# The up-products of MLP and feed-forward layers as 512-column products in two PSUM banks

## The chip, the core and the metric

The kernel runs on one core of one Trainium2 chip. A core has TensorE (PE in the profile; its weight loads are the separate row PEld), VectorE (DVE), ScalarE (ACT), GpSimd (POOL) and SyncE (SP), and DMA engines that bring data from memory. The metric is the time of one execution in microseconds on the device; less is better.

## The reference, cut to what matters

A stack of four blocks (a sequence mixer and an MLP each) is followed by two layers (feed-forward, hybrid mixer, cross attention, feed-forward), on 256 tokens of width 1024, all in float32. The change concerns the first product of each MLP and the gate and up products of each feed-forward:

```python
D_MODEL = 1024; SEQ = 256; D_FF = 4 * D_MODEL; D_FF_2 = 2816
def sq_relu_mlp(h, w1, w2):                      # four times, h is (256, 1024)
    return jnp.square(jax.nn.relu(h @ w1)) @ w2
def swiglu(h, w_gate, w_up, w_down):             # four times
    return (jax.nn.silu(h @ w_gate) * (h @ w_up)) @ w_down
    ...
for i in range(DEPTH):       # 4
    x = x + rms_norm(mixer(rms_norm(x, norm_g[i, 0])), norm_g[i, 1])
    h = rms_norm(x, norm_g[i, 2])
    x = x + rms_norm(sq_relu_mlp(h, mlp_w1[i], mlp_w2[i]), norm_g[i, 3])
for l in range(DEPTH_2):     # 2
    x = x + 0.5 * swiglu(rms_norm_2(x, ffn1_norm[l]), ffn1_w_gate[l], ffn1_w_up[l], ffn1_w_down[l])
    x = x + hybrid_mixer(...)
    x = x + memory_cross_attention(...)
    x = x + 0.5 * swiglu(rms_norm_2(x, ffn2_norm[l]), ffn2_w_gate[l], ffn2_w_up[l], ffn2_w_down[l])
```

## The kernel before

Activations lie with channels on the 128 partitions and the 256 tokens along the free side, as 8 chunks of 128 channels. To keep float32 accuracy with the faster number format of TensorE (fp32r), each operand is split in a high and a low part, and a product is the sum of three: high weights with high activations, high weights with low activations, low weights with high activations. Low with low is left out.

Weights stream through the core in slabs of 128 x 2048 numbers (1 MB). For each slab SP issues the DMA into `ring` (3 places; a place is free when the slab three before it has its low part, line 405), ACT copies it rounded into `wH` (line 1440; 2 places, free when the products of the slab two before are done, line 1439), and DVE takes the difference `wL` (line 2064). PE multiplies. The order on every engine is written out by hand in one function per layer kind, and semaphores join the engines: `high_split`, `low_split` (a slab's parts are there), `products_done` (its products are done), `bank_read` (its PSUM bank has been read).

An MLP has 16 up slabs and 16 down slabs, a feed-forward 22 up slabs (half gate, half up columns of 128) and 11 down slabs. The first two up slabs are done by `first_products`, in step with the arrival of the normalized activations; the change does not touch them. It touches slabs 2 to 15 of each of the four MLPs and slabs 2 to 21 of each of the four feed-forwards: 4 x 14 + 4 x 20 = 136 slabs. Each of them gives two column blocks of 128 channels x 256 tokens, which fill the halves of one PSUM bank (4 + j % 4). For each block `three` (line 602) issues 8 products high x high, 8 high x low, 8 low x high, each 256 columns wide with a weight load of its own: 48 products per slab.

Behind the product, in an MLP: ACT makes the ReLU of the bank into `act_s` (line 1578), DVE multiplies it with the bank into `prod_s` (the square, line 2175, which frees the bank), ACT rounds it to the high part of the hidden activations (line 1595), and DVE takes their low part (line 2164). In a feed-forward: DVE scales the bank by the row norm into `act_s` (line 2220, frees the bank), ACT makes SiLU of the gate half (line 1600), DVE multiplies the halves (line 2204), ACT rounds (line 1604), DVE takes the low part (line 2209). On ACT and DVE, the split of the slab two further on stands ahead of this work: in `ready` (line 1449) and `refill` (line 2075). The down products then use banks 0 to 3 (`down_product`).

## Time and profile before

| | |
|---|---|
| time, median of 3 runs | 2692.18 us (2687.8 to 2705.8) |
| span of the profiled execution | 2705.3 us (the longest of the three times, 2705.8, is 0.5 us above it) |
| PE busy | 2625.5 us, 97% of the span, 21582 products |
| weight loads busy | 2553.7 us, 94% |
| DVE busy | 1660.7 us, 61% |
| ACT busy | 1351.4 us, 50% |
| POOL busy | 152.2 us, 6% |
| chain that ended last | PE 85%, DVE 6%, ACT 4% |
| mean granted clock of TensorE | 0.993 |

The page gives busy time by engine, the busy share in 40 slices of the span, the DMA queues, the chain of work that ended last (followed back from the end), and the costliest groups of instructions with their mean duration and the idle time before them. A product of TensorE is pipelined: the time from one start to the next is what it costs in a row of products, and its own duration is longer.

### The profile page before, as it was taken

To read this page: it belongs to the slowest core of one execution; us is meant where nothing else is said; L and a number is where in the kernel's file an instruction comes from. 1 tells how busy PE (TensorE), PEld (TensorE's weight loads), DVE (VectorE), ACT (ScalarE), POOL (GpSimd) and SP (SyncE) were. 2 spreads that over 40 slices of the span, in tenths; PEclk is the share of its full clock that TensorE was granted. 3 is DMA by queue.
4 is the path that set the end of the run, shared out by engine and by line. 5 is a ranking of instruction groups with operands and counts; after the bars stand their busy time and mean duration, and the time that the engine had idled before them with its cause. 6 is when DMAs were issued, how large, how long until landed. Compare 5 with 4: busy or idle time off the path is not lost.

```text
span 2705.3 us, 48788 instructions
## 1 busy us (share of the span) xinstructions
PE 2625.5 (97%) x21582; PEld 2553.7 (94%) x21582; DVE 1660.7 (61%) x1970; ACT 1351.4 (50%) x1663; POOL 152.2 (6%) x224
## 2 busy tenths in 40 slices
PE   8989999999998999989999999999999999999998
PEld 8979999899997999988999999989999999999998
DVE  5657655475575754676755665766665657764664
ACT  5645545454436544663544444554545446544543
POOL 4400000000000000330000000000000000000000
PEclk9999999999999999999999999999999999999999
DMA  7514564456643565442565756434766655334663
GB/s 214 162 33 141 187 234 133 152 176 211 211 144 121 179 219 186 144 147 94 171 216 178 191 187 211 152 125 141 196 194 187 189 199 159 126 130 142 188 188 125
DMA packets 429970, 451.96 MB, mean 167 GB/s; under 512 B 13346, under 2 KB 395024, under 8 KB 427584
## 3 DMA queue, kind: packets, MB, share of 16 engines
q1 hardware_dynamic: 417952, 416.12, 49.2%
q0 software_dynamic: 7312, 32.35, 3.5%
q8 instruction: 170, 2.79, 0.4%
q10 hardware_dynamic: 4496, 0.39, 0.1%
q14 instruction: 40, 0.33, 0.0%
HBM read 441.21 MB, written 7.60 MB: 166 GB/s over the span
## 4 chain that ended last, share of the span: by engine, by line
PE 85%; DVE 6%; ACT 4%; POOL 2%; DMA 1%; issue 1%; ACTq 0%; SPq 0%; DVEq 0%
PE ps L593 85%; ACT wH L1440 2%; DVE wL L2064 2%; POOL arena L497 1%; ACT hidden_parts L1500 1%; PE ps L1037 0%; POOL arena L499 0%; DMA ring<-in_gdn_w_in 0%; DVE arena L2484 0%; DMA arena<-tiles_out 0%; DVE arena L2592 0%; DMA arena<-leaf_out 0%; DMA leaf_out<-arena 0%; POOL arena L507 0%; DVE arena L2335 0%
## 5 line engine op out<-in xcount | busy, mean ns | idle before, releaser
L2064 DVE TENSOR_TENSOR wL<-ring,wH 128x2048 fp32r<-128x2048 f32 x392 | 898.4, 2292 | 781.2 <-ACT wH L1440 780.8
L1440 ACT ACTIVATE wH<-ring 128x2048 fp32r<-128x2048 f32 x392 | 752.4, 1919 | 1050.6 <-PE ps L593 1048.6
L593 PE MATMUL ps<-hidden_parts,wH 128*128 128x256 f32 x6656 | 1005.0, 279 | 4.1 <-ACT hidden_parts L1500 2.7
L593 PEld LDWEIGHTS ps<-hidden_parts,wH 128*128 128x128 f32 x6656 | 910.8, 188 | 6.1 <-issue 3.6
L593 PE MATMUL ps<-hidden_parts,wL 128*128 128x256 f32 x3328 | 700.4, 279 | 1.0 <-DVE wL L2064 1.0
L593 PEld LDWEIGHTS ps<-hidden_parts,wL 128*128 128x128 f32 x3328 | 525.4, 188 | 1.4 <-DVE wL L2064 1.4
L593 PE MATMUL ps<-hH,wH 128*128 128x256 f32 x2624 | 369.5, 282 | 7.1 <-DVE hH L2081 5.0
L593 PE MATMUL ps<-hH,wL 128*128 128x256 f32 x2624 | 361.6, 279 | 2.2 <-DVE wL L2064 2.2
L593 PEld LDWEIGHTS ps<-hH,wH 128*128 128x128 f32 x2624 | 331.4, 189 | 16.6 <-issue 15.9
L593 PE MATMUL ps<-hL,wH 128*128 128x256 f32 x2624 | 347.0, 278 | 0.0
L593 PEld LDWEIGHTS ps<-hH,wL 128*128 128x128 f32 x2624 | 329.2, 189 | 2.9 <-DVE wL L2064 2.8
L593 PEld LDWEIGHTS ps<-hL,wH 128*128 128x128 f32 x2624 | 322.1, 188 | 0.0
L593 PE MATMUL ps<-arena 128*128 128x128 f32 (+1 forms) x1392 | 231.0, 312 | 21.1 <-ACT arena L1840 7.5
L593 PEld LDWEIGHTS ps<-arena 128*128 128x128 f32 x1392 | 197.0, 195 | 40.1 <-ACT arena L1840 10.2
L593 PE MATMUL ps<-sq,onesR 128*128 128x256 f32 (+1 forms) x216 | 71.8, 461 | 4.8 <-ACT sq L1516 2.8
L2320 DVE SCALAR_TENSOR_TENSOR hT<-hT,arena 128x255 f32<-128x255 f32 (+1 forms) x144 | 60.9, 492 | 3.7 <-ACT hT L1660 3.4
L2220 DVE TENSOR_TENSOR arena<-ps,rs 128x512 f32<-128x512 f32 x88 | 60.2, 684 | 0.1
L593 PEld LDWEIGHTS ps<-sq,onesR 128*128 128x128 f32 x216 | 37.3, 189 | 19.7 <-issue 8.0
L593 PE MATMUL ps<-hidden_parts 128*128 128x256 f32 x384 | 53.3, 291 | 0.0
L593 PEld LDWEIGHTS ps<-hidden_parts 128*128 128x128 f32 x384 | 49.0, 191 | 0.9
L2175 DVE TENSOR_TENSOR arena<-arena,ps 128x512 f32<-128x512 f32 x64 | 43.6, 681 | 5.9 <-ACT arena L1578 5.9
L1595 ACT ACTIVATE hidden_parts<-arena 128x512 fp32r<-128x512 f32 x64 | 40.1, 627 | 12.1 <-DVE arena L2175 12.1
(301 smaller groups left out, 1965.2 us busy)
## 6 DMA issues: line engine op xcount, KB each, us to landing
ring<-in_mlp_w SPq DMA_DIRECT2D x128, 1024.0 KB, 5.4
ring<-in_ffn_w_gate SPq DMA_DIRECT2D x88, 512.0 KB, 3.9
ring<-in_ffn_w_up SPq DMA_DIRECT2D x88, 512.0 KB, 5.2
ring<-in_ffn_w_down SPq DMA_DIRECT2D x44, 1024.0 KB, 5.0
ring<-in_gdn_w_in SPq DMA_DIRECT2D x32, 1024.0 KB, 5.9
ring<-in_w_in SPq DMA_DIRECT2D x28, 1024.0 KB, 5.4
hidden_parts<-mem_parts POOLq DMA_DIRECT2D x14, 1024.0 KB, 7.5
ring<-in_mlstm_w_in SPq DMA_DIRECT2D x12, 1024.0 KB, 5.2
```

The lines of the kernel that those rows point to most:

```text
L497: W.chain(pool.tensor_tensor(step, leafA[:, k, k + 1:LEAF][:, :, None].broadcast_to([P, n, c]), leafX[:, k, 0:c][:, None, :].broadcast_to( ...
L593: return pe.matmul(o, l, r, start=start, stop=stop, **k)
L1440: f(wH[:, n % PARTS, :], ring[:, n % RING, :], ACT.Copy).then_inc(sem("high_split"), 1)
L1500: ins = f(x_parts[0][:, k, :], xT[:, k, :], ACT.Copy, scale=column(gain, k0 + k))
L1595: f(hidH[:, 2 * g:2 * g + 2, :], two(prod_s[:, g % 2, :]), ACT.Copy).then_inc(sem("hiddenH_ready"), 1)
L2064: tt(wL[:, n % PARTS, :], ring[:, n % RING, :], wH[:, n % PARTS, :].bitcast(F32), ALU.subtract)\
L2175: tt(prod_s[:, g % 2, :], act_s[:, g % 2, :], ps[:, 4 + g % 4, :], ALU.mult)\
L2220: tt(two(act_s[:, n % 2, :]), two(ps[:, 4 + n % 4, :]), rs_twice(), ALU.mult)\
L2320: ins = stt(dst, src, w, dst, ALU.mult, ALU.add)
```

## The change

Slabs 2 and on of the up-products take two PSUM banks each, in turns of three pairs (0 and 1, 6 and 7, 4 and 5), one bank per column block. Bank halves no longer stand for column blocks: the left half collects high weights x high activations, the right half high weights x low activations. As both use the same weights, one product of 512 columns does both, with an operand that steps over the high and the low tensor (so `hH` and `hL` become the two halves of one tensor `normed`). The low weights then go over the high activations alone into the left half. A slab has 16 products of 512 columns and 16 of 256.

The halves must be added. In an MLP ACT copies the right halves out of both banks (in place of ReLU), DVE adds the left halves to the copy (frees the banks), and, after the low part of the slab before, makes max(x, 0) times x in one instruction from the sum. In a feed-forward ACT has a new copy of the right halves into `sum_s`, DVE has a new addition, and the scaling reads the sum. New semaphores tell that the square (`hidden_squared`) and the scaled units (`units_scaled`) are there. PE waits for the pair's bank_read from slab 5 on, for `hidden_squared` or `units_scaled` at slab 4, and for the banks of the last but one slab before the down product. The wait that the memory filler's bank (6) has been emptied stands at slab 3 in place of 2. The load of the identity at the start signals the semaphore of x. The core of the diff:

```diff
-        hH = sb("hH", [P, DC, T], F32R)
-        hL = sb("hL", [P, DC, T], F32R)
+        normed = sb("normed", [P, 2, DC, T], F32R)
+        hH, hL = normed[:, 0, :, :], normed[:, 1, :, :]
...
+        sum_s = A.take(2 * 512, "p (b n) -> p b n", b=2)
...
+        ffn_both = hidden_parts[:, :, 24:32, :]
...
+        def wide_banks(j):
+            return (0, 6, 4)[(j - 2) % 3]
+
+        def both_sums(j):
+            v = ps[:, wide_banks(j):wide_banks(j) + 2, :]
+            return v[:, :, 0:T], v[:, :, T:2 * T]
... PE
+            def wide_product(u, j, high_of, low_of, x):
+                for m in range(2):
+                    bank = wide_banks(j) + m
+                    halves = two(ps[:, bank, :])
+                    for k in range(DC):
+                        mm(halves, high_of(k, m), x[:, :, k, :], k == 0, False, skip_group_check=True)
+                    if m == 0:
+                        pe.wait_ge(sem("low_split"), u + 1)
+                    for k in range(DC):
+                        last = mm(ps[:, bank, 0:T], low_of(k, m), x[:, 0, k, :], False, k == DC - 1,
+                                  skip_group_check=True)
+                last.then_inc(sem("products_done"), 1)
... PE, mlp
                 for j in range(2, 16):
-                    if j == 2:
+                    if j == 3:
                         filler_out(filled_before[("mlp", i)])
-                    to_channels("mlp_w1", i, j, bank_of(j), free="bank_read")
+                    if j == 4:
+                        pe.wait_ge(sem("hidden_squared"), W.next("hidden_squared", 2))
+                    if j >= 5:
+                        pe.wait_ge(sem("bank_read"), W.next("bank_read"))
+                    u = slab_no[("mlp_w1", i, j)]
+                    wh, wl = high(u, DC), low(u, DC)
+                    wide_product(u, j, lambda k, m: columns(wh, k, m), lambda k, m: columns(wl, k, m), normed)
...
+                W.next("hidden_squared", 14)
+                pe.wait_ge(sem("bank_read"), W.next("bank_read", 2))
 
                 def floor():
-                    pe.wait_ge(sem("bank_read"), W.next("bank_read", 4))
+                    pe.wait_ge(sem("bank_read"), W.next("bank_read"))
                     norm_floor()
... ACT, mlp
-                    f(act_s[:, g % 2, :], ps[:, 4 + g % 4, :], ACT.Relu).then_inc(sem("act_ready"), 1)
+                    src = two(ps[:, 4 + g, :]) if g < 2 else both_sums(g)[1]
+                    f(two(act_s[:, g % 2, :]), src, ACT.Copy).then_inc(sem("act_ready"), 1)
... ACT, ffn
                     ready(kind, l, n)
+                    if n >= 2:
+                        f(two(sum_s[:, n % 2, :]), both_sums(n)[1], ACT.Copy).then_inc(sem("act_ready"), 1)
... DVE, mlp
-                    tt(prod_s[:, g % 2, :], act_s[:, g % 2, :], ps[:, 4 + g % 4, :], ALU.mult)\
-                        .then_inc(sem("bank_read"), 1)
+                    src = act_s[:, g % 2, :]
+                    if g >= 2:
+                        tt(two(src), both_sums(g)[0], two(src), ALU.add).then_inc(sem("bank_read"), 1)
                     if g >= 1:
                         hidden_low(g - 1)
+                    if g >= 2:
+                        dve.wait_ge(sem("bank_read"), W.next("bank_read"))
+                    stt(prod_s[:, g % 2, :], src, 0.0, src, ALU.max, ALU.mult).then_inc(sem("hidden_squared"), 1)
... DVE, ffn
-                    tt(two(act_s[:, n % 2, :]), two(ps[:, 4 + n % 4, :]), rs_twice(), ALU.mult)\
-                        .then_inc(sem("bank_read"), 1)
-                    dve.wait_ge(sem("bank_read"), W.next("bank_read"))
+                    src = ps[:, 4 + n, :] if n < 2 else sum_s[:, n % 2, :]
+                    if n >= 2:
+                        dve.wait_ge(sem("act_ready"), W.next("act_ready"))
+                        tt(two(src), both_sums(n)[0], two(src), ALU.add).then_inc(sem("bank_read"), 1)
+                        dve.wait_ge(sem("bank_read"), W.next("bank_read"))
+                    tt(two(act_s[:, n % 2, :]), two(src), rs_twice(), ALU.mult).then_inc(sem("units_scaled"), 1)
+                    dve.wait_ge(sem("units_scaled"), W.next("units_scaled"))
```

What stands in a row on PE for one up slab of the first MLP (slab 4), before:

```order
L593 MATMUL ps<-hH,wH 128x256 [waits mlp_bank_read,high_split]
L593 MATMUL ps<-hH,wH 128x256 x7
L593 MATMUL ps<-hL,wH 128x256 x8
L593 MATMUL ps<-hH,wL 128x256 [waits low_split]
L593 MATMUL ps<-hH,wL 128x256 x7
L593 MATMUL ps<-hH,wH 128x256 x8
L593 MATMUL ps<-hL,wH 128x256 x8
L593 MATMUL ps<-hH,wL 128x256 x8
```

and for the same slab now (`normed` holds hH and hL):

```order
L602 MATMUL ps<-normed,wH 128x512 [waits high_split,hidden_squared]
L602 MATMUL ps<-normed,wH 128x512 x7
L602 MATMUL ps<-normed,wL 128x256 [waits low_split]
L602 MATMUL ps<-normed,wL 128x256 x7
L602 MATMUL ps<-normed,wH 128x512 x8
L602 MATMUL ps<-normed,wL 128x256 x8
```

The six groups of eight became four, the wait for the low weights comes after 8 wide products in place of 16 narrow ones, and the wait for the bank is one for an event later in the work on DVE.

On DVE, up slabs 3 and 4 of the first MLP, before (line 2064 is the low part of a slab two further on, 2175 the square, 2164 the low part of the hidden activations):

```order
L2064 TENSOR_TENSOR wL<-ring,wH 128x2048 [waits high_split]
L2175 TENSOR_TENSOR arena<-arena,ps 128x512 [waits act_ready,hidden_ready]
L2164 TENSOR_TENSOR hidden_parts<-arena,hidden_parts 128x512 [waits hiddenH_ready]
L2064 TENSOR_TENSOR wL<-ring,wH 128x2048 [waits high_split]
L2175 TENSOR_TENSOR arena<-arena,ps 128x512 [waits act_ready,hidden_ready]
L2164 TENSOR_TENSOR hidden_parts<-arena,hidden_parts 128x512 [waits hiddenH_ready]
```

and now (2096 the low part of a slab, 2209 the addition, 2196 the low hidden part, 2214 the square):

```order
L2096 TENSOR_TENSOR wL<-ring,wH 128x2048 [waits high_split]
L2209 TENSOR_TENSOR arena<-ps,arena 128x512 [waits act_ready,hidden_ready]
L2196 TENSOR_TENSOR hidden_parts<-arena,hidden_parts 128x512 [waits hiddenH_ready]
L2214 SCALAR_TENSOR_TENSOR arena<-arena 128x512 [waits mlp_bank_read]
L2096 TENSOR_TENSOR wL<-ring,wH 128x2048 [waits high_split]
L2209 TENSOR_TENSOR arena<-ps,arena 128x512 [waits act_ready,hidden_ready]
```

One instruction of 128x512 has been added per slab, and the square now stands last. The release of PSUM stays where it was, directly behind the low part of the slab.

## Rows read from the trace of the kernel before

**Rows 1.** The page: busy time, and the chain that ended last.
```profile
PE 2625.5 (97%) x21582; PEld 2553.7 (94%) x21582; DVE 1660.7 (61%) x1970; ACT 1351.4 (50%) x1663; POOL 152.2 (6%) x224
...
PE ps L593 85%; ACT wH L1440 2%; DVE wL L2064 2%; POOL arena L497 1%; ACT hidden_parts L1500 1%; PE ps L1037 0%; POOL arena L499 0%; DMA ring<-in_gdn_w_in 0%; DVE arena L2484 0%; DMA arena<-tiles_out 0%; DVE arena L2592 0%; DMA arena<-leaf_out 0%; DMA leaf_out<-arena 0%; POOL arena L507 0%; DVE arena L2335 0%
```

**Rows 2.** Waits in total, times, longest (us).
```profile
ACT wH L1440 <- PE ps L593: 1048.6, 348, 6.8
DVE wL L2064 <- ACT wH L1440: 780.8, 333, 8.0
...
PE ps L593 <- DVE wL L2064: 5.0, 7, 1.6
```

**Rows 3.** Timeline, PE, first MLP, up slabs: start, length (us), count.
```profile
262.31 1.10 PE L593 MATMUL ps<-hH,wH 128*128 128x256 f32 x8
...
273.62 1.10 PE L593 MATMUL ps<-hH,wH 128*128 128x256 f32 x8
```

**Rows 4.** Timeline, second MLP, a steady up slab, three engines.
```profile
619.73 1.07 PE L593 MATMUL ps<-hH,wH 128*128 128x256 f32 x8
620.01 1.92 ACT L1440 ACTIVATE wH<-ring 128x2048 fp32r<-128x2048 f32 x1 [2.51 <-PE ps L593]
...
621.83 0.59 ACT L1578 ACTIVATE arena<-ps 128x512 f32<-128x512 f32 x1
621.97 2.29 DVE L2064 TENSOR_TENSOR wL<-ring,wH 128x2048 fp32r<-128x2048 f32 x1 [1.95 <-ACT wH L1440]
...
624.18 0.68 DVE L2175 TENSOR_TENSOR arena<-arena,ps 128x512 f32<-128x512 f32 x1
...
626.98 1.07 PE L593 MATMUL ps<-hH,wL 128*128 128x256 f32 x8
```

**Rows 5.** Windows of up phases: PE busy (count), clock, DMA share, GB/s.
```profile
267.00:327.00 60.00, 60.00 (x512) 1.00 0.58 186
585.00:645.00 60.00, 60.00 (x531) 1.00 0.61 195
...
1505.00:1565.00 60.00, 60.00 (x511) 1.00 0.70 192
1910.00:1970.00 60.00, 60.00 (x531) 1.00 0.71 194
```

**Rows 6.** Timeline, PE: 32 products of plain f32, each with other weights.
```profile
447.91 7.07 PE L593 MATMUL ps<-hT,gw 128*8 128x256 f32 x32
```

**Rows 7.** Groups by line, shapes apart: total us, mean ns of one, idle before.
```profile
L593 PE MATMUL ps<-arena 128*128 128x256 f32 x384 | 111.8, 397 | 13.5 <-ACT arena L1840 7.5 <-ACT arena L1554 2.6 <-DVE arena L2592 1.8
L2220 DVE TENSOR_TENSOR arena<-ps,rs 128x512 f32<-128x512 f32 x88 | 60.2, 684 | 0.1
...
L2204 DVE TENSOR_TENSOR arena<-arena 128x256 f32<-128x256 f32 x88 | 37.4, 425 | 7.7 <-ACT arena L1600 4.8
...
L1578 ACT ACTIVATE arena<-ps 128x512 f32<-128x512 f32 x64 | 36.9, 584 | 0.0
```

**Rows 8.** Timeline, end of the second MLP's up phase: ACT, then DVE.
```profile
652.09 0.63 ACT L1595 ACTIVATE hidden_parts<-arena 128x512 fp32r<-128x512 f32 x1 [1.95 <-DVE arena L2175]
...
652.94 1.91 ACT L1440 ACTIVATE wH<-ring 128x2048 fp32r<-128x2048 f32 x1
658.07 1.93 ACT L1440 ACTIVATE wH<-ring 128x2048 fp32r<-128x2048 f32 x1 [3.23 <-PE ps L593]
...
654.88 2.29 DVE L2064 TENSOR_TENSOR wL<-ring,wH 128x2048 fp32r<-128x2048 f32 x1 [1.09 <-ACT wH L1440]
```

**Rows 9.** Timeline, ACT, down slabs of a feed-forward and of the second MLP.
```profile
1612.27 1.92 ACT L1440 ACTIVATE wH<-ring 128x2048 fp32r<-128x2048 f32 x1 [2.92 <-PE ps L593]
1617.92 1.92 ACT L1440 ACTIVATE wH<-ring 128x2048 fp32r<-128x2048 f32 x1 [3.74 <-PE ps L593]
...
663.74 1.93 ACT L1440 ACTIVATE wH<-ring 128x2048 fp32r<-128x2048 f32 x1 [3.74 <-PE ps L593]
669.18 1.93 ACT L1440 ACTIVATE wH<-ring 128x2048 fp32r<-128x2048 f32 x1 [3.51 <-PE ps L593]
```

More of the change, by code:

```diff
@@ L152 @@
           "vec_in", "vec_turned", "masks_ready", "leaf_", "inverse_in",
-          "kv_", "memH_ready", "mem_normed", "act_ready", "hiddenH_ready", "hidden_ready", "o_ready", "prob_ready", "post_squared", "post_folded")
+          "kv_", "memH_ready", "mem_normed", "act_ready", "hiddenH_ready", "hidden_ready", "o_ready", "prob_ready", "hidden_squared", "units_scaled", "post_squared", "post_folded")
 VECTOR_SETUP = {"lambda_sums": 1, "lb_diff": 2, "lambda_ready": 3, "lb_ready": 4, "params_ready": 5}
@@ L206, in __init__ @@
             def __init__(self, eng, step):
-                self.eng, self.seen, self.step, self.steps = eng, {}, sem(step), 0
+                self.eng, self.seen, self.step, self.steps = eng, {}, step, 0
             def next(self, name, n=1):
@@ L216, in mark @@
                 self.steps += 1
-                ins.then_inc(self.step, 1)
+                ins.then_inc(sem(self.step), 1)
                 return self.steps
             def chain(self, ins):
-                self.eng.wait_ge(self.step, self.mark(ins))
+                self.eng.wait_ge(sem(self.step), self.mark(ins))
         def group(name, layer, j, g=0):
@@ L330, in program @@
         memH, memL = hidden_parts[:, 0, 24:32, :], hidden_parts[:, 1, 0:8, :]
-        ffn_x = (hidH[:, 24:32, :], hidL[:, 24:32, :])
+        ffn_both = hidden_parts[:, :, 24:32, :]
+        ffn_x = (ffn_both[:, 0, :, :], ffn_both[:, 1, :, :])
         cross_x = [flat_parts[:, at:at + DC * T].rearrange("p (c t) -> p c t", c=DC)
@@ L391, in _ @@
         def _(sp):
-            sp.dma_start(ident, io["shape_constants"][:, 0:P]).then_inc(sem("ident_in"), 16)
+            sp.dma_start(ident, io["shape_constants"][:, 0:P]).then_inc(sem("x_in"), 16)
             sp.dma_start(x_rows, io["x"][0].rearrange("(i p) n -> p i n", p=P)).then_inc(sem("x_in"), 16)
@@ L869, in ffn @@
                 for n in range(2, 22):
+                    if n == 3:
+                        filler_out(filled_before[(kind, l)])
+                    if n == 4:
+                        pe.wait_ge(sem("units_scaled"), W.next("units_scaled", 2))
+                    if n >= 5:
+                        pe.wait_ge(sem("bank_read"), W.next("bank_read"))
                     u = slab_no[(kind, l, n)]
                     wh, wl = high(u, 2 * DC), low(u, 2 * DC)
-                    if n == 2:
-                        filler_out(filled_before[(kind, l)])
-                    if n >= 4:
-                        pe.wait_ge(sem("bank_read"), W.next("bank_read"))
-                    for half in range(2):
-                        last = three(ps[:, 4 + n % 4, half * T:(half + 1) * T],
-                                     [lambda k: wh[:, half * DC + k, :], lambda k: wl[:, half * DC + k, :]],
-                                     [lambda k: ffn_x[0][:, k, :], lambda k: ffn_x[1][:, k, :]], DC,
-                                     low_weights(u, (1, 0)) if half == 0 else None)
-                    last.then_inc(sem("products_done"), 1)
+                    wide_product(u, n, lambda k, m: wh[:, m * DC + k, :], lambda k, m: wl[:, m * DC + k, :], ffn_both)
+                W.next("units_scaled", 20)
+                pe.wait_ge(sem("bank_read"), W.next("bank_read", 2))
                 down_product(f"{kind}_w_down_2", l, 22, range(22))
-                pe.wait_ge(sem("bank_read"), W.next("bank_read", 4))
+                pe.wait_ge(sem("bank_read"), W.next("bank_read"))
             def outputs(heads, values):
@@ L1403, in turn_in @@
                     last.then_inc(sem(name), 1)
-            pe.wait_ge(sem("ident_in"), W.next("ident_in", 16))
             pe.wait_ge(sem("ones_set"), W.next("ones_set"))
-            pe.wait_ge(sem("x_in"), W.next("x_in", 16))
+            pe.wait_ge(sem("x_in"), W.next("x_in", 32))
             turn_in(x_rows, "x_turned")
@@ L1593, in hidden_high @@
             def hidden_high(g):
-                act.wait_ge(sem("bank_read"), W.next("bank_read"))
+                act.wait_ge(sem("hidden_squared"), W.next("hidden_squared"))
                 f(hidH[:, 2 * g:2 * g + 2, :], two(prod_s[:, g % 2, :]), ACT.Copy).then_inc(sem("hiddenH_ready"), 1)
@@ L1598, in gate_unit @@
                 def gate_unit(n):
-                    act.wait_ge(sem("bank_read"), W.next("bank_read"))
+                    act.wait_ge(sem("units_scaled"), W.next("units_scaled"))
                     f(gate_s[:, n % 2, :], act_s[:, n % 2, 0:T], ACT.Silu).then_inc(sem("act_ready"), 1)
```

## The prediction

> **What bounds the kernel now.** I read the busy times and the chain first. PE is busy 97% of the span and holds 85% of the chain; nearly all of that is the one line that issues products [rows 1]. Next the waits: ACT waits 1048.6 us in all for PE before it splits a slab, DVE waits 780.8 us for ACT, while PE waits 5.0 us in all for low weights [rows 2]. So PE runs and the others follow it, and in the up phases only a cheaper stream of products can shorten the span.
>
> How much does a product cost? The timeline merges eight of one kind into a row; the distance of starts is the price. In the first MLP twelve rows of eight lie between 262.31 and 273.62 us: 11.31 us for 96 products, 117.8 ns each [rows 3]. In the second MLP eight rows lie between 619.73 and 626.98 us: 7.25 us for 64, 113.3 ns each [rows 4]. The granted clock is 1.00 in both (2.4 GHz, at which 256 columns alone take 106.7 ns), so there are two rates at one clock, and I have no reason for the choice between them. The windows show that a phase keeps its rate: about 512 products in 60 us in four of the eight up phases (both outer MLPs, the first and the last feed-forward), about 531 in the other four [rows 5]. A slab of 48 is then 5.65 or 5.44 us. The down phases show the same two periods on ACT, 1612.27 to 1617.92 and 663.74 to 669.18 [rows 9]. Weight loads run beside the products, one for each, and are busy 94% of the span [rows 1]. So a narrow product costs 6.6 to 11.1 ns above its columns, and the load of the next weights is the likely reason: it cannot start before the product ahead of it has taken over its own weights.
>
> **The products.** Columns don't change: 48 x 256 = 16 x 512 + 16 x 256. What goes is 16 products and 16 weight loads in each of 136 slabs, 2176 of 21582. A 512-column product of this format is nowhere in the trace. The nearest row is 32 products of plain f32 with 256 columns, each with other weights: 7.07 us from the first start to the last end [rows 6]. Taking 0.397 us off for the last one's own length, the mean of plain f32 products of this width [rows 7], leaves 6.67 us for 31 steps, 215.3 ns each. That is 2 ns above 512 columns at 2.4 GHz (213.3), as if plain f32 went over its 256 columns twice, so one streams as long as the new wide product does. I take 216 ns. The 16 products with low weights stay narrow, at 113.3 or 117.8.
>
> Slab at the slow rate: 16 x 0.216 + 16 x 0.1178 = 5.34 us, against 5.65: 0.31 saved. Slab at the fast rate: 3.46 + 1.81 = 5.27 against 5.44: 0.17 saved. With 68 slabs of each, as four phases of eight show, 68 x 0.31 + 68 x 0.17 = 32.6 us.
>
> The other bound of the wide product: that the 6.6 to 11.1 ns belong to every product, whatever its width. Then it costs 219.9 or 224.4 ns, and a slab saves 16 times 6.7 or 11.2 ns, 0.11 or 0.18 us: 19.6 us in all. I take 216, since [rows 6] has weight changes too. A page of the Trainium skill speaks against the change here. "TensorE: Matmul & The Clock Gate", section "Back-to-back issue gap", gives N/2.4 + 2.5 ns. By that, 256 columns cost 109.2 ns and 512 cost 215.8, and the change would save 16 x 2.6 ns a slab, 5.7 us in all. The rows agree with it for the long products (215.3), and disagree for these narrow ones (113.3 and 117.8), so the measured prices stand in the sum.
>
> **The work behind the products.** Within a slab's period DVE has the split of 2.29 us, the square 0.68 and the low part, of the same shape, 0.68 [rows 4, 7], 3.65 us. The change adds one instruction of 128x512, by the rows 0.68: 4.33 in an MLP. In a feed-forward the scaling 0.684, two pieces of half the width (0.425) and the addition 0.68 beside the split make 4.5 [rows 7]. Both are under 5.27. ACT gains 0.58 per slab in a feed-forward and nothing in an MLP (a copy for a ReLU of the same shape). That adds 136 x 0.68 = 92 us to DVE and 80 x 0.58 = 46 us to ACT, off the path as long as four points hold.
>
> Low weights: they are ready when ACT has started the split 0.28 us after PE's next slab begins (620.01 against 619.73), and DVE has ended 4.25 us later (624.26) [rows 4], 4.5 us after that slab's start. PE wants them 5.3 us (one slab) and 8 x 0.216 = 1.7 us after it: 2.5 us of slack. Banks: the addition ends at about 624.9, 5.1 us after the start, and three pairs rotate, so PE wants the pair after two slabs or more, 10.5 us. Even the first such wait, on the square of slab 1, stands ahead of the split of slab 4's low weights on DVE, for which PE waits in any case. The filler wait at slab 3 and the identity's semaphore cost nothing; bank 6 is emptied long before and x is needed with the identity. DMA: 1 MB in 5.27 us is some 200 GB/s, at a DMA share of 0.6 to 0.7 now at 186 to 195 [rows 5]. I see no bound there. The start of the down product waits for the addition of slab 14: ready 5.1 us after slab 15 began, wanted after 5.27 to 5.34. It fits by 0.2 us.
>
> The fourth point costs something: the end of an up phase. ACT makes the last high part (652.09) only when DVE has the square, and splits down slab 2 behind it (652.94); DVE ends its low part at 657.17. PE begins that slab about 0.28 us before 658.07 and wants low weights two products later, at 658.0 [rows 8]. The slack is 0.8 us. Now the last square comes after an addition and a low part in place of alone, 1.36 us later: a wait of about 0.5 us at the fast rate and 0.1 at the slow, and in a feed-forward, with 0.7 us more delay, some 0.3. For eight phases 2.5 us. At the beginning of an up phase DVE lags (the 5.0 us of waits [rows 2]); the first slab or two can't give their saving, about 0.3 us in each of eight phases, 2.4 us. Together 5 us, between 1 and 10.
>
> **The sum** against the profiled span: 2705.3 - 32.6 + 5 = 2677.7. The median is 2692.2, 13 us under that span. If that is fewer slabs at the slow rate (0.21 us each, some 60 slabs), about 30% of slabs rather than half are slow in a median run. Then the saving is 136 x (0.3 x 0.31 + 0.7 x 0.17) = 28.8, less 5: 24. Forecast: 2692 - 24 = 2668.
>
> **The rivals.** (1) The rate locks. The wide products may reset how loads and products interlock, and phases keep what they begin with, the 64 + 44 = 108 down slabs too. All fast: the narrow 16 of each up slab at the slow share gain 0.3 x 136 x 0.07 = 3, the down slabs 0.3 x 108 x 0.21 = 7: 2658. All slow: 0.7 x 136 x 0.07 = 7 and 0.7 x 108 x 0.21 = 16 lost: 2691. For it: [rows 3, 4, 9] show rates that persist over phases. Against: nothing shows a width that sets them.
>
> (2) The fixed price is every product's. Saving in the median's mix 136 x (0.3 x 0.18 + 0.7 x 0.11) = 18, less 5: 2679. For it: it explains two rates without weight loads. Against: [rows 6].
>
> (3) Slower: the wide product's operand steps between two tensors (the second run begins 8 or 32 KB on), and each run could cost like a product of its own, started anew. No product of the trace reads two runs, so the only bound is the price of two products plus a penalty. It decides from 2 x 114.7 = 229.4 ns less 5 us over 2176, 227 ns. At 240 ns, 5% over two narrow ones, the products lose 2176 x 0.0106 = 23 us, and with the 5 the time is 2720. Against: PE would have to feel a step in an address that it makes anyway.
>
> (4) DVE becomes the bound. Decides when its work per slab passes 5.3 us, so with 0.8 us of handovers beyond the 4.5. Each 0.1 us above costs 14 us, 2690 to 2710. Against: the present records follow each other without gaps, 621.97, 624.18 [rows 4].
>
> That the change doesn't do what it says is excluded by the order of instructions, which shows the wide products.
>
> **Chances.** Forecast 0.55 (own range 2655 to 2680), rates all fast 0.10, all slow 0.08, fixed price 0.15, slower by (3) or (4) 0.12. 1% is 26.9 us, about what a measurement of this kernel can tell from no change; it lies at 2665.3, inside the forecast's range. Of the forecast 0.26 is below it, and with the fast lock and a few of the rest faster is 0.38, slower 0.08, and the rest 0.54 is within 1%. Range: 2650 to 2692.
>
> **What would show it.** Steady up slabs with a period of ACT's split of 5.27 or 5.34 us; eight wide products 1.73 us apart from the next row. 19406 products on the page. DVE busy up by 92, ACT by 46. PE's wait for low weights grown by a few us at the first down slabs. I am wrong if a wide product costs 220 ns or more, if down slabs change their mix of 5.44 and 5.65, or if PE waits for DVE in steady slabs.

## The result and the profile after

The changed kernel takes 2705.13 us (median of 20 runs, 2695.54 to 2717.49), the kernel before 2694.55 (20 runs, 2683.75 to 2706.49): a ratio of 1.0033, with a 95% interval of 1.0019 to 1.0048. So in this comparison it is slower by a third of a per cent: 9 us by the ratio, 10.6 by the two medians. The forecast was 2668, 24 us faster, with a range of 2650 to 2692. A second comparison on another chip (experiment 6) finds no difference, so what is firm is that the forecast gain is not there.

The profiled execution took 2702.61 us, its span is 2700.9 us, 4 us below the span of before: one execution, and the one of before was among its slowest. Below are lines of the page, and then the waits (us in total, times, longest):

```profile
PE 2623.0 (97%) x19406; PEld 2451.4 (91%) x19406; DVE 1749.9 (65%) x2106; ACT 1389.9 (51%) x1743; POOL 151.2 (6%) x224
...
PE ps L602 84%; ACT wH L1469 2%; DVE wL L2096 2%; ACT hidden_parts L1529 1%; PE ps L1067 1%; DMA ring<-in_gdn_w_in 0%; DVE arena L2524 0%; DVE arena L2632 0%; POOL arena L508 0%; POOL arena L506 0%; DVE arena L2375 0%; POOL arena L473 0%; DVE arena L2368 0%; ACT arena L1872 0%; DMA arena<-tiles_out 0%
```

```profile
ACT wH L1469 <- PE ps L602: 1002.2, 349, 7.0
DVE wL L2096 <- ACT wH L1469: 685.6, 334, 8.2
...
PE ps L602 <- DVE wL L2096: 7.1, 10, 1.6
```

The picture is that of [rows 1, 2]: PE bounds, the others wait. There are 2176 products fewer, as foreseen, yet PE is busy for only 2.5 us less. The eight up phases, each taken from its first product's start to its last one's, add up to 743.0 us in the trace of before and to 743.0 us in this one; with the down phases the sums are 1298.6 and 1296.8 us. A steady up slab of the second MLP (timeline: start, length, count), which answers to [rows 4]:

```profile
599.93 2.02 PE L602 MATMUL ps<-normed,wH 128*128 128x512 f32 x8
601.60 0.68 DVE L2209 TENSOR_TENSOR arena<-ps,arena 128x512 f32<-128x512 f32 x1
601.79 1.07 PE L602 MATMUL ps<-normed,wL 128*128 128x256 f32 x8
602.20 0.68 DVE L2196 TENSOR_TENSOR hidden_parts<-arena,hidden_parts 128x512 fp32r<-128x512 f32 x1
602.70 2.02 PE L602 MATMUL ps<-normed,wH 128*128 128x512 f32 x8
602.80 0.69 DVE L2214 SCALAR_TENSOR_TENSOR arena<-arena 128x512 f32<-128x512 f32 x1
602.98 1.93 ACT L1469 ACTIVATE wH<-ring 128x2048 fp32r<-128x2048 f32 x1 [2.63 <-PE ps L602]
604.94 2.29 DVE L2096 TENSOR_TENSOR wL<-ring,wH 128x2048 fp32r<-128x2048 f32 x1 [1.46 <-ACT wH L1469]
608.53 1.93 ACT L1469 ACTIVATE wH<-ring 128x2048 fp32r<-128x2048 f32 x1 [2.63 <-PE ps L602]
```

Eight wide products cost 601.79 - 599.93 = 1.86 us, 232.5 ns each; eight narrow ones 602.70 - 601.79 = 0.91 us, 113.8 ns. ACT's split has a period of 5.55 us (602.98 to 608.53), midway between the 5.44 and the 5.65 of before. DVE is done with a slab long before PE is; it binds nothing here. The starts of the single records refine the price (a step is the time from one start to the next): the first wide product behind a narrow one takes a step of 226 ns, the others 231 and 236 in turns, mean 232.7, and this in all eight phases. The narrow ones behind them begin with one step of 118 and then run at 113.3. The windows of the feed-forwards, which answer to [rows 5] (PE busy and count, clock, DMA share, GB/s), say the same of longer stretches: 60 us hold 346 to 350 products, 60 / 348 = 172.4 ns in the mean, (232.7 + 113.3) / 2 = 173.0.

```profile
1500.00:1560.00 60.00, 60.00 (x350) 1.00 0.69 190
1910.00:1970.00 60.00, 60.00 (x348) 1.00 0.69 189
...
2545.00:2605.00 60.00, 60.00 (x346) 1.00 0.68 188
```

The end of an up phase answers to [rows 8]. Timelines of the second MLP (ACT, DVE, PE), and of the first feed-forward (DVE, PE):

```profile
647.89 0.63 ACT L1625 ACTIVATE hidden_parts<-arena 128x512 fp32r<-128x512 f32 x1 [3.16 <-DVE arena L2214]
648.74 1.91 ACT L1469 ACTIVATE wH<-ring 128x2048 fp32r<-128x2048 f32 x1
650.68 2.29 DVE L2096 TENSOR_TENSOR wL<-ring,wH 128x2048 fp32r<-128x2048 f32 x1 [1.09 <-ACT wH L1469]
652.63 0.39 PE L602 MATMUL ps<-hidden_parts,wH 128*128 128x256 f32 x2
653.02 0.38 PE L602 MATMUL ps<-hidden_parts,wL 128*128 128x256 f32 x1
653.24 0.41 PE L602 MATMUL ps<-hidden_parts,wH 128*128 128x256 f32 x2
```

```profile
1602.40 2.29 DVE L2096 TENSOR_TENSOR wL<-ring,wH 128x2048 fp32r<-128x2048 f32 x1 [1.39 <-ACT wH L1469]
1603.86 0.39 PE L602 MATMUL ps<-hidden_parts,wH 128*128 128x256 f32 x2
1604.75 0.38 PE L602 MATMUL ps<-hidden_parts,wL 128*128 128x256 f32 x1 [0.49 <-DVE wL L2096]
```

The low part of down slab 2 ends at 652.97, and PE, two products into that slab, goes on at 653.02: in place of 0.23 us between these rows (as elsewhere in the slab) there are 0.39, and the next step is 0.11 longer too, 0.27 in all. In the feed-forward the low part ends at 1604.69, and the step is 0.89 us in place of 0.23, 0.77 with the next. All eight phases show one or the other of these (four times some 0.27, four times 0.77: 4.2 us). The kernel before has neither. The list of waits shows only 2.1 us of it (7.1 in place of 5.0 for low weights), since a product's record of 0.28 us counts as busy past its step.

### The profile page after: what moved, and what is told of

It is laid out like the page before. It is cut to its first block, busy times and chain, and to the rows that moved or that the text cites. A ratio compares the mean times of both kernels' runs of the same rounds, so it can differ in the third digit from the quotient of the medians.

```text
span 2700.9 us, 44656 instructions
## 1 busy us (share of the span) xinstructions
PE 2623.0 (97%) x19406; PEld 2451.4 (91%) x19406; DVE 1749.9 (65%) x2106; ACT 1389.9 (51%) x1743; POOL 151.2 (6%) x224
## 4 chain that ended last, share of the span: by engine, by line
PE 85%; DVE 7%; ACT 5%; issue 1%; POOL 1%; DMA 1%; ACTq 0%; SPq 0%; DVEq 0%
PE ps L602 84%; ACT wH L1469 2%; DVE wL L2096 2%; ACT hidden_parts L1529 1%; PE ps L1067 1%; DMA ring<-in_gdn_w_in 0%; DVE arena L2524 0%; DVE arena L2632 0%; POOL arena L508 0%; POOL arena L506 0%; DVE arena L2375 0%; POOL arena L473 0%; DVE arena L2368 0%; ACT arena L1872 0%; DMA arena<-tiles_out 0%
## 5 line engine op out<-in xcount | busy, mean ns | idle before, releaser
L602 PE MATMUL ps<-hidden_parts,wH 128*128 128x256 f32 (+1 forms) x5376 | 999.7, 305 | 3.6 <-ACT hidden_parts L1529 2.5
L602 PEld LDWEIGHTS ps<-hidden_parts,wH 128*128 128x128 f32 x5376 | 828.2, 188 | 48.3 <-issue 3.4
L602 PE MATMUL ps<-normed,wH 128*128 128x256 f32 (+1 forms) x4352 | 674.2, 305 | 6.4 <-DVE normed L2113 4.7
L602 PEld LDWEIGHTS ps<-normed,wH 128*128 128x128 f32 x4352 | 578.9, 189 | 46.1 <-issue 15.5
L602 PE MATMUL ps<-normed,wL 128*128 128x256 f32 x2624 | 360.9, 279 | 1.9 <-DVE wL L2096 1.9
L602 PEld LDWEIGHTS ps<-normed,wL 128*128 128x128 f32 x2624 | 336.9, 189 | 13.4 <-DVE wL L2096 3.7
L602 PE MATMUL ps<-wH,normed 128*128 128x256 f32 x512 | 66.8, 281 | 0.0
L602 PEld LDWEIGHTS ps<-wH,normed 128*128 128x128 f32 x512 | 62.4, 188 | 1.4 <-issue 1.4
L2261 DVE TENSOR_TENSOR arena<-arena,rs 128x512 f32<-128x512 f32 x80 | 55.3, 692 | 2.8
L2259 DVE TENSOR_TENSOR arena<-ps,arena 128x512 f32<-128x512 f32 x80 | 54.7, 684 | 0.0
```

What stands on the lines that cost most here:

```text
L602: return pe.matmul(o, l, r, start=start, stop=stop, **k)
L2259: tt(two(src), both_sums(n)[0], two(src), ALU.add).then_inc(sem("bank_read"), 1)
L2261: tt(two(act_s[:, n % 2, :]), two(src), rs_twice(), ALU.mult).then_inc(sem("units_scaled"), 1)
```

## The experiments

Three theories on the 232.7 ns stood after the result. A: the second run of the wide operand costs (a run is a stretch of numbers that lie side by side; the operand has two). B: this format (fp32r) costs more per column than plain f32. C: contention with the copies and DMAs of the full kernel makes wide products dear.

**1 and 2. The prices alone.** A kernel of its own, with rows of 96 products of one kind; each kind twice; then the same with ACT, DVE and the DMA queues kept busy.

```diff
+ for i in range(96): mm(weights[:, i % 16, :], run1[:, i % 8, 0:T], T)            # 256 columns
+ for i in range(96): mm(weights[:, i % 16, :], run1[:, i % 8, :], 512)            # 512, one run
+ for i in range(96): pe.matmul(two(ps[:, i % 2, :]), weights[:, i % 16, :],
+                               run2[:, :, i % 8, :], start=True, stop=True)       # 512, two runs
+ ... 256 in two runs of 128; 128; 384; plain f32 256; bf16 512; bf16 256; 8 wide and 8 narrow in turns
```

> A kernel of its own, no part of the reference: rows of 96 products of TensorE, each with other 128x128 weights than the one ahead, ACT, DVE and DMA idle beside them. The forms: fp32r of 256 columns; 512 columns in one run; 512 in two runs of 256 that lie 8 KB apart; 256 in two runs of 128; 128; 384; plain f32 of 256; bf16 of 512 and 256; eight of 512 and eight of 256 in turns. If the second run costs (theory A, my rival 3): 512 in one run 216 ns from start to start, 512 in two runs 226 to 236, 256 in two runs some 118 to 125. If the price goes with the columns of fp32r (theory B): both 512 forms 226 to 236, 384 some 170 to 177, 128 at 107 or more by its weight load, bf16 of 512 at 216. If other engines or DMAs make the narrow and the wide product dear (theory C): 216 for all 512 and 109 for all 256 here.

> The same rows of products, with ACT copying 128x2048, DVE subtracting 128x2048 and DMAs of 1 MB, two at a time, running beside the first half or more of them. Theories A and B: each form costs as in the quiet kernel within 1 ns. Theory C: dearer here than in the quiet kernel, 113 or 118 for 256 fp32r columns and 226 to 236 for 512.

Measured: 371.25 us quiet, 372.57 busy. Timelines, quiet and then busy, where the fp32r rows are the ones with operands in two runs (512 columns, then 256; the one-run kinds share one line of the kernel and merge in the view):

```profile
67.98 22.03 PE L95 MATMUL ps<-run,weights 128*128 128x512 f32 x96
89.99 11.76 PE L99 MATMUL ps<-run,weights 128*128 128x256 f32 x96
150.69 20.67 PE L79 MATMUL ps<-run_bf,weights_bf 128*128 128x512 bf16 x94
171.33 10.64 PE L79 MATMUL ps<-run_bf,weights_bf 128*128 128x256 bf16 x96
```

```profile
69.07 22.03 PE L97 MATMUL ps<-run,weights 128*128 128x512 f32 x96
91.08 11.76 PE L101 MATMUL ps<-run,weights 128*128 128x256 f32 x96
```

and a window of the busy kernel (PE, weight loads, DVE, ACT, POOL, each with its count; clock, DMA share, GB/s):

```profile
60.00:120.00 60.00, 60.00 (x373) 54.68 (x372) 59.12 (x27) 59.02 (x32) 0.00 (x0) 1.00 0.97 302
```

A row of 96 is 95 steps and the length of its last product: (22.03 - 0.39) / 95 = 228 ns and (11.76 - 0.28) / 95 = 121 ns, with a first step that is longer than the others. The starts of the single records give the settled steps in ns, the same in both kernels within 0.1:

| | 128 | 256 | 384 | 512 columns |
|---|---|---|---|---|
| fp32r, one run | 111.7 | 120.0 | 173.3 | 226.7 |
| fp32r, two runs | | 120.0 | | 226.7 |
| bf16 | | 109.2 | | 215.8 |
| plain f32 | | 215.8 | | |

The granted clock is 1.00, at which 256, 384 and 512 columns stream in 106.7, 160.0 and 213.3 ns. So an fp32r product of 256 or more columns costs 13.3 ns above its columns, whatever its width. A falls (two runs cost what one does), and C (nothing changes beside copies and a DMA share of 0.97). B falls as it was put: the extra is a price of the product and not of the column. By these prices the change turns 3 x 120.0 into 226.7 + 120.0 and would save 13.3 ns a pair, 16 x 13.3 = 213 ns a slab, 29 us. The kernel before doesn't pay 120.0 for its narrow products, though, but 113.3 or 117.8 [rows 3, 4]. And A, B and C leave open why the full kernel pays 232.7 for a wide product that costs 226.7 here. The Trainium skill, "TensorE: Matmul & The Clock Gate", section "Back-to-back issue gap", puts a product at N/2.4 + 2.5 ns. The bf16 rows agree with it to 0.1 ns (109.2, 215.8), the fp32r rows don't.

**3. One run for the wide operand in the full kernel.** The tensor of the MLPs is laid out so that a wide product reads 512 numbers in a row; the feed-forwards keep their two runs.

```diff
-        normed = sb("normed", [P, 2, DC, T], F32R)
+        normed = sb("normed", [P, DC, 2, T], F32R)
```

> The changed kernel with high and low activations side by side for each chunk (normed is 128 x 8 x 2 x 256), so that the wide products of the four MLPs read one run of 512 columns; those of the feed-forwards still read two. Theory A (the second run costs): in MLP up slabs the wide products go from 232.7 ns to 216, a slab from 5.56 us to 5.29, 56 slabs make 15 us: 0.994 of the changed kernel, just under the kernel before. Theory B (columns): 232.7 ns stays, and the time is that of the changed kernel, about 1.003 of the kernel before.

Measured: 2704.18 us (2697.34 to 2712.89), 0.9978 of the kernel before on that chip (2709.51; interval 0.9959 to 0.9998). Its timeline:

```profile
605.67 2.02 PE L602 MATMUL ps<-normed,wH 128*128 128x512 f32 x8
607.53 1.07 PE L602 MATMUL ps<-normed,wL 128*128 128x256 f32 x8
```

1.86 us again, 232.7 ns from the single starts, as in its feed-forwards. A is out in the full kernel as well. The time is 1 us from the changed kernel's 2705.13; what turns the ratio is the kernel before, which came out 15 us later on this chip than in the first comparison.

**4. The same work behind, narrow products.** Each wide product as two narrow ones; banks, additions and waits as in the changed kernel.

```diff
-                        mm(halves, high_of(k, m), x[:, :, k, :], k == 0, False, skip_group_check=True)
+                        for h in range(2):
+                            mm(halves[:, h, :], high_of(k, m), x[:, h, k, :], k == 0 and h == 0, False, ...)
```

> The changed kernel with each 512-column product issued as two of 256 columns (high weights x high activations, then the same high weights x low activations), so 48 products per slab again, with all of the changed work on ACT and DVE, the bank pairs and the waits. If the wide product gives nothing (what the two traces say: 232.7 ns against 2 x 113.3 or 117.8) this is as slow as the changed kernel within 0.2%, 1.003 of the kernel before, and the loss is the work and the waits behind the products. If the wide products themselves cost the time, it is back at 1.000.

Measured: 2706.52 us (2699.86 to 2718.53), ratio 0.999 (0.9973 to 1.0006). Timeline of the second MLP, and windows of the first and the last feed-forward:

```profile
605.76 1.98 PE L602 MATMUL ps<-normed,wH 128*128 128x256 f32 x16
607.57 1.07 PE L602 MATMUL ps<-normed,wL 128*128 128x256 f32 x8
```

```profile
1500.00:1560.00 60.00, 60.00 (x512) 1.00 0.68 187
2545.00:2605.00 60.00, 60.00 (x532) 1.00 0.71 194
```

Sixteen narrow products in 1.81 us are 113.1 ns each here, and in the first feed-forward 60 / 512 = 117.2: the two rates are back, some phases at one and some at the other, as in the kernel before. The time is 2 us from the one-run version's on the same chip (2704.18) and not told apart from it. Wide products against narrow ones, all else equal, neither gain nor lose that a median shows. The expectation's test (1.003 of the kernel before or 1.000) can't decide, since the kernel before had moved.

**5. What the price hangs on.** Rows of 96 narrow and wide products with other banks, sums of eight, the kernel's layouts, the kernel's order of operands, constant weights, constant activations, and half a weight load.

```diff
+ ... slab[:, i % 8, 0:P], run2[:, 0, i % 8, :], start=i % 8 == 0, stop=i % 8 == 7      # layouts, sums of eight
+ ... weights[:, 0, :] ...                                                             # one set of weights
+ pe.matmul(ps[0:64, 2, 0:T], weights[:, i % 16, 0:64], run1[:, i % 8, 0:T], ...)       # half a load
+ ... 8 wide (slab), then 8 narrow (slab_l) into the left half of the same bank, in turns
```

> A kernel of its own again, all else idle: rows of 96 products of fp32r with a mark between rows. The quiet kernel gave 120.0 ns for 256 columns, 173.3 for 384, 226.7 for 512: the columns at 2.4 GHz and 13.3 ns on top, whatever the width, and 215.8 for plain f32 of 256 and bf16 of 512. In the full kernel a narrow one costs 113.3 or 117.8 and a wide one 226 to 236. Theory D, the price is that of a weight load beside a product: with 64 weight columns in place of 128 it falls from 13.3 to about 7, for both widths. Theory E, it belongs to the instruction in this format: 13.3 stays with half a load. What makes the 113.3 of the full kernel: sums over eight products in one bank (then the row with these sums shows it and the row of starts does not), the kernel's way of laying out weights or activations (then it comes with those rows), or a phase between loads and products that an earlier wait sets (then all rows alike show 120).

Measured (timeline; 418.01 us): sums of eight, the same with the kernel's layouts, half a load narrow and wide, then the mixture:

```profile
57.19 11.76 PE L95 MATMUL ps<-run,weights 128*128 128x256 f32 x96
80.67 11.76 PE L101 MATMUL ps<-run,slab 128*128 128x256 f32 x96
171.62 11.71 PE L119 MATMUL ps<-run,weights 128*64 128x256 f32 x96
183.31 22.28 PE L122 MATMUL ps<-run,weights 128*64 128x512 f32 x96
...
211.24 2.00 PE L126 MATMUL ps<-run,slab 128*128 128x512 f32 x8
213.08 1.11 PE L128 MATMUL ps<-run,slab_l 128*128 128x256 f32 x8
214.03 2.00 PE L126 MATMUL ps<-run,slab 128*128 128x512 f32 x8
```

Every narrow row is at 120.0. Half a load leaves the price of a narrow product where it is (120.0) and makes a wide one dearer (229.9 in place of 226.7), so the length of the load is not what a product waits for. Every row still has one load per product, also the row with constant weights, so what a load costs as such is not shown. The mixture alone comes near the changed kernel: 214.03 - 211.24 = 2.79 us for 8 wide and 8 narrow, two of which make a slab of 5.58, against 5.55 in the kernel. The sums agree to 0.03 us, the parts do not: the wide ones take 230 ns here (236 down to 226 within a group of eight) and the narrow ones 119, where the kernel has 232.7 and 113.3. So the slab of the changed kernel costs about what these products cost by themselves. Three narrow products alone would cost 360 ns, a slab of 5.76; the slabs of before, at 5.44 or 5.65, are cheaper than that in a way that these rows don't show.

**6 and 7. The changed kernel again, and the change in the MLPs only**, on one chip.

```diff
 (feed-forwards)
-                    wide_product(u, n, lambda k, m: wh[:, m * DC + k, :], lambda k, m: wl[:, m * DC + k, :], ffn_both)
+                    for half in range(2):
+                        last = three(ps[:, 4 + n % 4, half * T:(half + 1) * T], ...)
```

> The changed kernel itself, unchanged, beside its rivals on one chip: on the first chip it was 1.0033 (1.0019 to 1.0048) of the kernel before; the one-run and split-wide kernels were at 0.998 and 0.999 on a second chip where the kernel before ran at 2709.5. If the chip made that difference, this is at about 0.998 to 1.000 on a chip with that time of before, and the width plays no part; if the wide two-run products cost something, it is at 1.003 on any chip.

> The change in the four MLPs alone; the feed-forwards as before. If nothing is gained in products and each phase loses a fixed wait at its end, this lies half way between the kernel before and the changed kernel, within 0.15% of both. If the loss were DVE's or ACT's in the feed-forwards, this would equal the kernel before.

Measured: the changed kernel 2702.97 (2698.89 to 2711.4), ratio 0.9996 (0.9979 to 1.0013) against 2705.26 for the one before; MLPs only 2698.77 (2691.5 to 2704.74), ratio 0.9978 (0.9961 to 0.9994). The changed kernel repeats itself to 2 us (2705.13 and 2702.97), while the kernel before has medians of 2694.55, 2709.51, 2705.26 and 2706.72 in four sets (the last is that of experiments 9 and 10). The loss of the first comparison is not found again. The MLPs-only version was expected within 0.15% of both and half way between them; it is 0.2% faster than the kernel before. In the trace of the MLPs-only version the four ends of feed-forwards have no wait for low weights, those of the MLPs have their 0.27 us: 4 x 0.77 = 3 us of the 4.2 us between the two versions.

**8. What chooses the rate.** Rows of 64 narrow and of 32 wide products behind waits of different length, and narrow rows behind one product of another kind.

```diff
+ for i in range(count): last = of(i)
+ last.then_inc(s_row, 1)
+ pe.wait_ge(s_go, row + 1)          # ACT: a copy of 64, 96, ... 288 columns after s_row
```

> A kernel of its own for the open question of what chooses between 113.3, 117.8 and 120.0 ns for one and the same narrow fp32r product, and why a wide one costs 232.7 ns in the changed kernel and 226.7 in the quiet rows. Rows of 64 narrow products, each behind a wait of PE for ScalarE that is a little longer each time (copies of 64 to 288 columns, in steps of 32), the same with rows of 32 wide products, twice; then rows of narrow products behind a single product of another kind (one wide, two wide, 128 columns, 384 columns, plain f32 of 128 and of 256 columns). Theory S (the moment at which a row starts after a stall chooses the rate, which the row then keeps): behind stalls some rows run at 113.3 or 117.8 ns and others at 120.0, each constant over its 64 products, and wide rows fall apart too, between 226.7 and some 233 ns. Theory K (the rate is set by what only the kernel has: its banks, its neighbours on the chip, its weights): every narrow row stays at 120.0 and every wide one at 226.7. Theory N (a product of another kind ahead of the row chooses): rows behind stalls stay at 120.0, and the rate changes behind some of the single products.

Measured (timeline; 412.22 us; the bracket is PE's idle time):

```profile
40.75 7.93 PE L84 MATMUL ps<-run,weights 128*128 128x256 f32 x64 [0.35 <-ACT back_h L71]
90.99 7.93 PE L84 MATMUL ps<-run,weights 128*128 128x256 f32 x64 [0.51 <-ACT back_h L71]
107.35 7.55 PE L84 MATMUL ps<-run,weights 128*128 128x512 f32 x32 [0.35 <-ACT back_h L71]
```

All narrow rows take 7.93 or 7.94 us. Their first steps are 221, 119, 118, 125, 113, 119 ns, then 120 for good; wide rows begin with a long step, then 231, 235, 229, 232, 231, 227, and settle at 226.7; behind single products of other kinds the rows return to a mean of 120 too. So theories S and N find nothing here, and 113.3 and 117.8 as settled rates were seen only in the full kernels, as K has it.

That doesn't exclude S. The waits of 0.34 to 0.53 us changed little: 14 of 16 narrow rows begin with the same steps to 1 ns. And the traces of the full kernels show what S says. In the kernel before, the first MLP's down phase changes its rate at a wait (timeline, and windows ahead of it and behind it):

```profile
379.66 0.39 PE L593 MATMUL ps<-hidden_parts,wL 128*128 128x256 f32 x1 [0.82 <-DVE wL L2064]
```

```profile
345.00:375.00 30.00, 30.00 (x257) 1.00 0.66 231
383.00:408.00 25.00, 25.00 (x223) 1.00 0.71 234
```

That is 117 ns a product, then 112 (117.8 and 113.3 from the single starts). In the eight traces of full kernels every change of rate within an up or a down phase lies across such a break: a wait, a step of 138 ns or more, or wide products. A break doesn't fix the rate, it lets it change. The changed kernel has the same wait of 0.27 us at the start of the second MLP's down phase in both of its traces, and goes on at the fast rate in the first and at the slow one in the second (window 656:716, first the trace of the result, then that of experiment 6):

```profile
656.00:716.00 60.00, 60.00 (x532) 1.00 0.72 253
656.00:716.00 60.00, 60.00 (x512) 1.00 0.68 244
```

**9 and 10. Longer groups.** The beginning of the wide rows suggested that 231 to 236 are the price of a group's first products. So: sixteen wide products, then sixteen narrow ones, in the whole kernel and in the MLPs-only version.

```diff
                 for m in range(2):
-                    bank = wide_banks(j) + m
...
-                    if m == 0:
-                        pe.wait_ge(sem("low_split"), u + 1)
+                pe.wait_ge(sem("low_split"), u + 1)
+                for m in range(2):
+                    bank = wide_banks(j) + m
```

> The changed kernel with the 16 wide products of a slab in one group (both banks), then the 16 narrow ones with low weights; nothing else moved. In the rows by itself a wide product right after a stall cost 231, 235, 229, 232, 231, 227 ns and then 226.7 for good; in the changed kernel groups of eight run at 231 and 236 in turns. Theory T (the excess over 226.7 belongs to the first products of a group): the last ten of sixteen cost 227, the mean is some 229 ns, a slab takes 5.49 us in place of 5.55, and the time falls by 8 us against the changed kernel's 2703 to 2705, to some 2696, ratio to the kernel before near 0.997. Theory K (the price belongs to the kernel, whatever the length of the group): all sixteen stay at 231 to 236, mean 232.7 to 233.5, the slab stays at 5.55 to 5.56 us. Both: PE waits for low weights, 7.1 us in all in the changed kernel, fall to some 3 us, since the wait now comes 3.7 us into a slab and not 1.9, so by K the time falls by some 3 us.

> The version with the change in the MLPs only (0.9978 of the kernel before, 2698.8 us), with the same grouping of 16 wide and 16 narrow products. Theory T: 56 slabs save 0.06 us each, 3.4 us, and with the waits for low weights 4.5: 2694, ratio 0.996. Theory K: 1 us for the waits alone, 2698, ratio 0.9975, no difference that this can measure.

Measured: 2704.49 us (2698.19 to 2712.54), ratio 0.9985 (0.9969 to 1.0002); MLPs only 2697.68 (2693.8 to 2702.21), ratio 0.995 (0.993 to 0.997), both against 2706.72. Timeline of the first:

```profile
603.49 3.89 PE L602 MATMUL ps<-normed,wH 128*128 128x512 f32 x16
607.22 1.98 PE L602 MATMUL ps<-normed,wL 128*128 128x256 f32 x16
609.04 3.19 PE L602 MATMUL ps<-normed,wH 128*128 128x512 f32 x13
```

3.73 us for sixteen, 233.1 ns each, with 231 and 236 in turns to the last: theory T falls, and K, the price of the full kernel whatever the length of the group, stands. The slab keeps its 5.55 us (603.49 to 609.04). The waits for low weights did not fall to 3 us, as both theories had it, but stayed at 7.1: the 4.2 us at the ends lie in down slabs, which this edit doesn't touch. The MLPs-only version is the fastest of all (0.995), but it isn't told apart from the one without the regrouping (0.9978), since their intervals meet and the sets are on two chips. Both lie below the kernel before with their whole intervals, a small gain that no expectation had and that stays unexplained.

## Why the prediction was wrong

**What bounds the kernel** was right: PE, and a cheaper stream of products would have been seen in the time. DVE gained 89 us of busy time and ACT 38.5 (92 and 46 forecast), and neither shows in a steady slab. Rival 4 is out.

**The step that failed** is "I take 216", the price of a wide product from [rows 6], the products of plain f32. It costs 232.7 in the kernel. 216 is right for what [rows 6] show, plain f32 of 256 columns (215.8 alone), and for bf16 of 512; it doesn't carry over to fp32r, where a wide product costs 226.7 even alone. 16.7 ns over 2176 products are 36 us, more than the whole forecast saving of 28.8. Of the 16.7, the format explains 10.7 (226.7 - 216); why the full kernel adds 6.0 stays open.

**The reason given** for the narrow products' excess, the load of the next weights, found no support: half a load changes nothing for narrow products alone (experiment 5). Rival 2, "the fixed price is every product's", comes nearest, at a chance of 0.15, but took the price from the rates in the kernel, 6.6 to 11.1 ns, where products alone show 13.3 and the wide ones in the kernel 19.4 (232.7 - 213.3). With 19.4, a pair of one wide and one narrow product costs 346.0 ns against 3 x 113.3 = 340 or 3 x 117.8 = 353: a slab loses 0.11 us where it was fast and gains 0.10 where it was slow. I had written down "I am wrong if a wide product costs 220 ns or more", and that is what came. Rival 3 names a break-even of 227 ns with two runs as the cause; the price passed the point, the cause is excluded by experiments 1 and 3.

**The mix of rates.** The changed up slabs are all at 5.55, and the narrow products in them at 113.3, so rival 1 came in part: the wide products fix the rate of the products behind them, within the up phases. The down phases keep both rates (a down phase of an MLP takes 76.3 or 79.3 us from its first start to its last in the traces of after). The reading that a phase keeps its rate holds while nothing breaks the stream; behind a wait it may change (experiment 8), and the change puts a wait of its own at the start of each down phase. Of 100 down slabs in one piece, 52 are at the slow rate in the trace of before, 23 in that of after and 36 when it was run again. With one execution of before traced, this can't tell whether the mix has moved, which was one of the three signs of being wrong.

In the up slabs the change gains or loses by what the kernel before has: with a share s of slow slabs, 136 x (0.11 - 0.21 s) us. In the trace of before half of them are slow, so this is near nothing, as measured (743.0 and 743.0 us). With the same half, the forecast had 32.6 us saved, less 2.4 at the beginnings.

The step from the span to the median rests on a guess that the record doesn't bear out: that the 13 us between the profiled execution and the median were slabs at the other rate, so that 30% of slabs are slow in a median run. By s = 0.3 the change would lose 6.4 us and 4 more at the ends, near the loss of the first comparison; but s was counted in no median run. In the eight traces of full kernels the up and down phases take 1293 to 1299 us in all, and the rest of the span, which the change hardly touches, 1400 to 1413. So the scatter of single executions lies more outside the phases than in them, and neither the loss in the first comparison nor the medians of the kernel before (2694.55 to 2709.51) are shown to come from the rates. They stay open.

**The ends of up phases** cost 4.2 us and the beginnings next to nothing: 5 in the forecast, of which 2.5 for the ends and 2.4 for the beginnings. The place and the mechanism were right, the MLPs' 0.27 us lie in the forecast's 0.1 to 0.5, the feed-forwards' 0.77 us were put at 0.3. Banks, the start of the down product and the steady low weights cost nothing, as expected.

## What to carry to other kernels

Price an instruction that is nowhere in the trace by itself on the chip, in its own format, before counting on it: the nearest row had the right number of passes and the wrong format, and the difference of 17 ns was larger than the gain. Fusing products of the same weights saved at best the fixed price of one product here, 13 ns in 360; and where a kernel's stream already runs below the price of its products alone, even that may be gone. The median of one and the same kernel moved by 15 us between sets, more than the difference to be read: compare several times, on more than one chip, before reading a third of a per cent, and compare the touched stretches in the traces, where 743.0 us stood against 743.0.

## What the runs showed of the hardware

Alone, an fp32r product of 256 to 512 columns costs its columns at 2.4 GHz and 13.3 ns (120.0, 173.3, 226.7); 128 columns of fp32r cost 111.7. A bf16 product costs its columns and 2.5 ns (109.2 for 256, 215.8 for 512), and plain f32 of 256 columns as much as bf16 of 512 (215.8). Two runs of an operand, 8 KB apart, cost what one does. Half a weight load costs a narrow product the same as a whole one and a wide product 3 ns more.

One and the same narrow product settles at 120.0 ns alone and at 113.3 or 117.8 in the up and down phases of the full kernels, and a wide one at 226.7 alone and at 231 and 236 in turns there. Within these phases the narrow rate changed only across a break of the stream, and not at every break. Banks, sums, layouts and the neighbours ACT, DVE and DMA were tried on products alone and don't make the difference; waits of 0.34 to 0.53 us there didn't either, but nearly all of these led to the same first steps. What chooses the rate stays open. A version that held all phases at 113.3 was not found.
